# One stage instead of three behind the recurrent branch, and eight table loads moved from the opening stage into the first norm's stage

## The reference, cut to what matters

```
def rwkv_output(y, prep, r_k, gn_w, gn_b):
    r, k_mod, v, g = prep[0], prep[1], prep[2], prep[6]
    mu = jnp.mean(y, axis=-1, keepdims=True)
    var = jnp.mean(jnp.square(y - mu), axis=-1, keepdims=True)
    yn = ((y - mu) * lax.rsqrt(var + GN_EPS)).reshape(B, L, RWKV_WIDTH) * gn_w + gn_b
    coef = ...                      # one number per token and head
    bonus = (coef[..., None] * v.reshape(B, L, RWKV_HEADS, RWKV_HEAD)).reshape(B, L, RWKV_WIDTH)
    return (yn.astype(r.dtype) + bonus) * g       # g = sigmoid(gl) @ g2
```

## Time and profile before

| | |
|---|---|
| median of 3 runs | 3859.2 us (3856.57 to 3866.98) |
| the profiled execution's own time | 3855.86 us |
| its span, first to last instruction | 3854.0 us |
| TensorE busy | 3429.4 us (89%) |
| VectorE busy | 1710.8 us (44%) |
| ScalarE busy | 976.4 us (25%) |
| mean granted TensorE clock | 0.938 of full speed |

### The profile page before, as it was taken

The page is one execution under the profiler, slowest core; times in us unless marked ns, Lnnn a source line. Parts: engine busy times, 40 slices in busy tenths (PEclk is TensorE's granted clock), DMA queues, the critical chain, the costliest instruction groups (busy, mean ns, idle before and its releaser), DMA issues. The chain is left out here.

```text
span 3854.0 us, 66346 instructions
## 1 busy us (share of the span) xinstructions
PE 3429.4 (89%) x28910; PEld 2721.4 (71%) x28910; DVE 1710.8 (44%) x2845; ACT 976.4 (25%) x1671; POOL 38.9 (1%) x48
## 2 busy tenths in 40 slices
PE   5969997997988999996989977899999978979998
PEld 3858995766867655554845845788887867868877
DVE  3655554563155111113544437544443256555643
ACT  3035441242222111112111133311112132533322
POOL 0000000000000000000000000000000000000000
PEclk8969997998998899998999988999999989999999
DMA  6130002503255799994531100144432111013332
GB/s 241 61 137 4 4 4 97 192 23 111 83 181 196 303 410 411 410 414 155 181 113 49 55 14 22 61 115 121 125 114 72 61 31 50 1 45 99 98 105 87
DMA packets 254322, 486.84 MB, mean 126 GB/s; under 512 B 12394, under 2 KB 148107, under 8 KB 245364
## 3 DMA queue, kind: packets, MB, share of 16 engines
q1 hardware_dynamic: 246964, 457.91, 34.1%
q0 software_dynamic: 1984, 16.81, 1.1%
q10 hardware_dynamic: 5120, 8.39, 0.6%
HBM read 453.68 MB, written 29.39 MB: 125 GB/s over the span
## 5 line engine op out<-in xcount | busy, mean ns | idle before, releaser
L398 PE MATMUL banks<-leading,w_rest 128*128 128x512 f32 (+2 forms) x2016 | 733.8, 364 | 60.2 <-DVE w_rest L335 59.6
L398 PE MATMUL banks<-rest,w_leading 128*128 128x512 f32 (+2 forms) x2016 | 722.9, 359 | 0.0
L398 PE MATMUL banks<-leading,w_leading 128*128 128x512 f32 (+2 forms) x2016 | 721.2, 358 | 0.0
L335 DVE TENSOR_TENSOR w_rest<-land,w_leading 128x1024 fp32r<-128x1024 f32 (+2 forms) x344 | 321.7, 977 | 518.1 <-ACT w_leading L320 518.1
L398 PEld LDWEIGHTS banks<-leading,w_rest 128*128 128x128 f32 (+1 forms) x2016 | 383.5, 190 | 132.9 <-DVE w_rest L335 40.0
L320 ACT CAST w_leading<-land 128x1024 fp32r<-128x1024 f32 (+2 forms) x344 | 275.7, 849 | 709.1 <-DMA land<-in_w_in 245.1
L398 PEld LDWEIGHTS banks<-leading,w_leading 128*128 128x128 f32 (+1 forms) x2016 | 383.0, 190 | 57.4
L398 PEld LDWEIGHTS banks<-rest,w_leading 128*128 128x128 f32 (+1 forms) x2016 | 384.1, 191 | 54.1
L398 PE MATMUL banks<-w_rest,leading 128*128 128x512 f32 (+3 forms) x772 | 297.2, 385 | 51.6 <-DVE w_rest L335 51.6
L398 PE MATMUL banks<-w_leading,rest 128*128 128x512 f32 (+3 forms) x772 | 292.0, 378 | 0.0
L398 PE MATMUL banks<-w_leading,leading 128*128 128x512 f32 (+3 forms) x772 | 290.6, 376 | 0.0
(11 more groups left out here) (586 smaller groups left out, 5080.8 us busy)
## 6 DMA issues: line engine op xcount, KB each, us to landing
wg<-in_w_exp_gate SPq DMA_DIRECT2D x32, 2048.0 KB, 12.7
wu<-in_w_exp_up SPq DMA_DIRECT2D x32, 2048.0 KB, 14.8
wd<-in_w_exp_down SPq DMA_DIRECT2D x32, 2048.0 KB, 11.8
ws<-in_ada_w SPq DMA_DIRECT2D x96, 512.0 KB, 3.8
land<-in_w_in SPq DMA_DIRECT2D x41, 1024.0 KB, 5.5
land<-in_ffn_up SPq DMA_DIRECT2D x44, 512.0 KB, 5.3
land<-in_ffn_up SPq DMA_DIRECT2D x88, 256.0 KB, 3.3
ws<-in_w_ada SPq DMA_DIRECT2D x32, 512.0 KB, 3.8
```

The costliest lines, as they stand in the source:

```text
L335: nc.vector.tensor_tensor(rest[s % 2][:, k0:k1, 0:n], slots[s % wslots][:, k0:k1, 0:n], leading[s % 2][:, k0:k1, 0:n].bitcast(F32), ALU.su ...
L398: mm = nc.tensor.matmul(bank_of(r, kind, at), lhsT, rhs, start=(k == 0 and q == 0), stop=(k == kt - 1 and q == len(each) - 1))
```

## The change

The three result stages become one. What each engine's list holds now:

- TensorE: the four bonus products, then (after `g2` has landed) the four gate products, then, after VectorE has read the bonus products and normed `y`, the 16 transposes, head pair by head pair (four pieces fill one bank).
- VectorE: mean and centring in two halves of 1024 values, the sums of squares in two halves, then the four bonus multiplications, the scaling by `rstd` in two halves, and per head pair an addition and the gate multiplication.
- ScalarE: the squares in two halves (before, VectorE multiplied), the root, and the reading of the transposed heads with scale `gn_w` and bias `gn_b`, 128x512 at a time.
- GpSimd: both loads of `hT` one behind the other, and the wait for both.
- SyncE: the load of `g2`, for which TensorE now waits itself.

In the opening, SyncE no longer issues the eight tables; it does so at the start of its list in the first norm's stage and then waits for them.

```
@@ opening
                 bring_ahead(m, sp)
-                for dst, src in later:
-                    sp.dma_start(dst[:], src).then_inc(m.tables_sem, 16)
-                m.tables_count = 16 * len(later)
+                m.later_tables = later
@@ block_one
+        def tables(sp):
+            for dst, src in m.later_tables:
+                sp.dma_start(dst[:], src).then_inc(m.tables_sem, 16)
+            sp.wait_ge(m.tables_sem, 16 * len(m.later_tables))
...
-                   lambda sp: sp.wait_ge(m.tables_sem, m.tables_count), m.first_sums)
+                   tables, m.first_sums)
@@ rwkv_result
+        halves_of = [slice(groups * q, groups * (q + 1)) for q in range(2)]
...
             @block.gpsimd
-                pool.dma_start(m.hT[0][:, :, :], m.hT_dram[0]).then_inc(m.back, 16)
+                for part, x in enumerate(m.hT):
+                    pool.dma_start(x[:, :, :], m.hT_dram[part]).then_inc(m.back, 16)
+                pool.wait_ge(m.back, 32)
...
+            @block.tensor
+                for p in range(KB):
+                    mm = nc.tensor.matmul(m.ps[:, 4 + p, :], m.headspread[0:RH, p, :], m.coef[0:RH, :], start=True, stop=True)
+                    mm.then_inc(made_sem, 1)
+                pe.wait_ge(landed_sem, 16)
+                for p in range(KB):
+                    nc.tensor.matmul(m.ps[:, p, :], b.g2[:, p * P:(p + 1) * P], m.rw[:, 14, CTX:TOK], start=True, stop=True).then_inc(made_sem, 1)
+                pe.wait_ge(scaled_sem, KB)
+                pe.wait_ge(normed_sem, 2)
+                for h in range(KB):
+                    for t in range(NTL):
+                        mm = nc.tensor.transpose(m.ps[:, 4 + h, t * P:(t + 1) * P], m.y[:, t, h * P:(h + 1) * P], m.ident)
+                    mm.then_inc(turned_sem, 1)
             @block.scalar
+                for q, own in enumerate(halves_of):
+                    act.wait_ge(centred_sem, q + 1)
+                    nc.scalar.activation(b.sq[:, own, :], y[:, own, :], ACT.Square).then_inc(squared_sem, 1)
                 act.wait_ge(summed_sem, 1)
                 nc.scalar.activation(b.root[:, :], b.ss[:, :], ACT.Sqrt).then_inc(rooted_sem, 1)
+                for h in range(KB):
+                    act.wait_ge(turned_sem, h + 1)
+                    nc.scalar.activation(m.br_rw[:, h, :], m.ps[:, 4 + h, :], ACT.Identity, bias=gb[:, h:h + 1], scale=gw[:, h:h + 1]).then_inc(taken_sem, 1)
```

More of the change, by code:

```diff
@@ L1936, in rwkv_result @@
             nc, ctx, mean=[NTL * RH, 1], ss=[NTL * RH], root=[NTL * RH], rstd=[NTL * RH, 1], sq=[NTL * RH, HD], g2=[512], t=[KB, LAT])
+        groups = NTL * RH // 2
+        halves_of = [slice(groups * q, groups * (q + 1)) for q in range(2)]
         y = m.y[:].rearrange("p t (h e) -> p (t h) e", e=HD)
-        n = NTL * RH
-        with stage(nc, landed=1, summed=1, rooted=1, chain=1) as (block, landed_sem, summed_sem, rooted_sem, chain_sem):
+        gw, gb = cols(m, "gn_w"), cols(m, "gn_b")
+        with stage(nc, landed=1, centred=1, squared=1, summed=1, rooted=1, made=1, scaled=1, normed=1, turned=1, taken=1, chain=1) as (
+                block, landed_sem, centred_sem, squared_sem, summed_sem, rooted_sem, made_sem, scaled_sem, normed_sem, turned_sem, taken_sem, chain_sem):
             @block.gpsimd
             def _(pool):
-                pool.dma_start(m.hT[0][:, :, :], m.hT_dram[0]).then_inc(m.back, 16)
+                for part, x in enumerate(m.hT):
+                    pool.dma_start(x[:, :, :], m.hT_dram[part]).then_inc(m.back, 16)
+                pool.wait_ge(m.back, 32)
             @block.sync
@@ L1946, in _ @@
                 sp.dma_start(b.g2[:, :], a["gate_w2"]).then_inc(landed_sem, 16)
-                sp.wait_ge(landed_sem, 16)
+            @block.tensor
+            def _(pe):
+                for p in range(KB):
[10 more added lines that the diff above has]
+                    mm.then_inc(turned_sem, 1)
             @block.scalar
             def _(act):
+                for q, own in enumerate(halves_of):
+                    act.wait_ge(centred_sem, q + 1)
+                    nc.scalar.activation(b.sq[:, own, :], y[:, own, :], ACT.Square).then_inc(squared_sem, 1)
                 act.wait_ge(summed_sem, 1)
                 nc.scalar.activation(b.root[:, :], b.ss[:, :], ACT.Sqrt).then_inc(rooted_sem, 1)
+                for h in range(KB):
+                    act.wait_ge(turned_sem, h + 1)
+                    nc.scalar.activation(m.br_rw[:, h, :], m.ps[:, 4 + h, :], ACT.Identity, bias=gb[:, h:h + 1], scale=gw[:, h:h + 1]).then_inc(taken_sem, 1)
             @block.vector
@@ L1956, in _ @@
                 chain = Chain(dve, chain_sem)
[L1957 to L1961, removed]
+                for own in halves_of:
+                    chain(nc.vector.tensor_reduce(b.mean[:, own, 0], y[:, own, :], AX, ALU.add))
+                    chain(nc.vector.tensor_scalar(b.mean[:, own, 0], b.mean[:, own, 0], 1.0 / HD, None, ALU.mult))
+                    nc.vector.tensor_tensor(y[:, own, :], y[:, own, :], bc(b.mean[:, own, :], HD), ALU.subtract).then_inc(centred_sem, 1)
@@ L1962, in _ @@
+                for q, own in enumerate(halves_of):
+                    dve.wait_ge(squared_sem, q + 1)
+                    chain(nc.vector.tensor_reduce(b.ss[:, own], b.sq[:, own, :], AX, ALU.add))
                 nc.vector.tensor_scalar(b.ss[:, :], b.ss[:, :], 1.0 / HD, GN_EPS, ALU.mult, ALU.add).then_inc(summed_sem, 1)
+                for p in range(KB):
+                    dve.wait_ge(made_sem, p + 1)
+                    nc.vector.tensor_tensor(b.t[:, p, :], m.ps[:, 4 + p, :], m.rw[:, 8 + p, CTX:TOK], ALU.mult).then_inc(scaled_sem, 1)
@@ L1963, in _ @@
                 dve.wait_ge(rooted_sem, 1)
                 chain(nc.vector.reciprocal(b.rstd[:, :, 0], b.root[:, :]))
[L1965 to L1988, removed]
@@ new lines, in _ @@
+                for own in halves_of:
+                    nc.vector.tensor_tensor(y[:, own, :], y[:, own, :], bc(b.rstd[:, own, :], HD), ALU.mult).then_inc(normed_sem, 1)
+                dve.wait_ge(made_sem, 2 * KB)
+                dve.wait_ge(scaled_sem, KB)
+                for h in range(KB):
+                    dve.wait_ge(taken_sem, h + 1)
+                    chain(nc.vector.tensor_tensor(b.t[:, h, :], b.t[:, h, :], m.br_rw[:, h, :], ALU.add))
+                    chain(nc.vector.tensor_tensor(m.br_rw[:, h, :], b.t[:, h, :], m.ps[:, h, :], ALU.mult))
```

## The result

The changed kernel takes 3838.95 us (median of 4 runs, 3838.54 to 3840.92) against 3860.61 us for the kernel before (4 runs, 3856.57 to 3866.98): ratio 0.9943, 95% interval 0.9931 to 0.9955. Measured a second time (experiment 10) it took 3840.88 us beside 3861.29, ratio 0.9949 (0.9936 to 0.9963). The medians differ by 21.7 and 20.4 us. The two profiled executions, 3855.86 us before and 3839.17 after, differ by 16.7.

What follows compares the result with a forecast made beforehand. Bound: barriers waiting for SyncE's tables in the opening and the result stages' serial chain. -3.5 - 16.2 = -19.7 us gives 3836.2 from the profiled time, 3839.5 from the median; forecast 3838, range 3829 to 3848.

Steps and rivals of the forecast that it cites:

- Part 1: Opening: moving SyncE's eight table issues into the first norm's stage starts that stage 3.5 us earlier, loads covered there.
- VectorE's path: Result stage: norm in halves, bonus multiplications and scaling end at 636.4 us, when the transposes may start.
- TensorE's path: Result stage: eight bonus and gate products, the clock falling at 624.5, end at 636.8 us, at most 638.9.
- as low as 630: Result stage: TensorE's products end this early if the clock stays up or comes back during the four gate products.
- Rival B: Result stage: clock stays low, TensorE is the bound, transposes from 638.9; in all -17.7 us, about 3840; chance 0.10.
- The pair of loads: Result stage: GpSimd's two hT loads, one behind the other, the second landing at 644.5 us, bounds 642.8 to 647.0.
- the lower bound's reading: Pair of hT loads: if the copy's 1 MB neighbour was all in between, the second load lands at 642.8 us.
- Rival A: Result stage: the two loads don't overlap, land at 647.0 and are the bound; -17.2 us, about 3840.5; chance 0.20.
- The wait that was hidden becomes the last one: Result stage's end: loads and VectorE end within half a microsecond, 644.5 against 644.2, so the load wait comes last.
- Rival C: Opening: the tables don't pay, 0 us for moving them; 3842 to 3843 us; chance 0.08.
- E: Whole kernel: nothing measurable, since waits elsewhere soak up the gain; chance 0.07.
- D: Result stage: g2 lands behind the pair and delays the gate products; slower once it lands after 648.6; chance 0.03.

Runs made afterwards that it cites:

- experiment 10: The changed kernel once more, unchanged, on the same chip as experiment 9; 3840.88 us, ratio 0.9949.
- experiment 2: The changed kernel with the eight table loads put back at the end of the opening; 3842.99 us, ratio 0.9953.
- experiment 5: The changed kernel with SyncE instead of GpSimd issuing the two 3 MB loads, right behind the g2 load; 3840.66 us, ratio 0.9947.
- experiment 6: The changed kernel with VectorE reading the transposed heads from the banks itself and ScalarE adding the bias to the bonus earlier; 3843.5 us, ratio 0.9956.
- experiment 7: The changed kernel with both edits: SyncE issues the two loads and VectorE reads the banks itself; 3839.82 us, ratio 0.9945.
- experiment 1: The kernel before with only the eight table loads moved into the first norm's stage; 3857.11 us, ratio 0.9993.
- experiment 8: The changed kernel with g2 issued by GpSimd as a third load behind the two 3 MB loads; 3853.36 us, ratio 0.9979.
- experiment 4: The kernel before once more, unchanged, for a second profile; 3857.99 us.
- experiment 9: The kernel of experiment 7 once more, beside the changed kernel on the same chip; 3841.49 us, ratio 0.995.
- experiment 3: The changed kernel with the bonus and gate products, and VectorE's bonus multiplications, placed behind the transposes; 3847.12 us, ratio 0.996.

## Why the prediction was right

The predicted 3838 us is 1 us from the 3838.95 measured, and the range (3829 to 3848) holds it. That nearness is partly luck. The gain by the medians is 21.7 us, not 19.7, the kernel before came out 1.4 us above the median I started from, and I had put the forecast between its profiled time and that median. What held is the mechanism and the size of each part. Step by step, in us from the start of the result stage:

| Step | predicted | measured |
|---|---|---|
| Tables out of the opening | -3.5 | -3.4 (means of 3 and 9 profiles) |
| Sums of squares done | 8.0 | 7.9 |
| Scaling done | 13.6 | 12.95 |
| TensorE's products done | 13.8 (7.2 to 16.1) | 8.95 |
| VectorE's last part begins | 15.6 | 14.75 |
| VectorE's last part | 5.8 | 5.75 |
| VectorE ends | 21.4 | 20.50 |
| Second load landed | 21.7 (20.0 to 24.2) | 20.6 |
| Barrier | 0.9 | 0.74 |
| Stage | 22.6 | 21.24 |

- **Part 1** held as written. The wait goes, the loads go under the norm's stage, and that stage does not get longer.
- **VectorE's path** held to 0.9 us. The four bonus multiplications follow each other at 0.60 us, not the 0.69 of a single row (629.40 to 631.79), and the two scalings take 2.36, not 2.5.
- **TensorE's path was mis-sized**, though it did not set the end. I let the clock fall at 624.5, as it had in the earlier trace rows with TensorE idle. With the bonus products running it stayed at full (2.4 GHz) until about 624.9, was at half until about 628.3, and came back during the gate products, as the windows in the last section show: the case that the prediction named with "as low as 630". The price at half clock was too high as well: I took 2.01 us from products that alternate between the two kinds, and products of one kind behind each other take 1.70 (last section). Rival B, in which it stays down, did not come about: the products were done 4 us before VectorE let the transposes go (2.45 us before in experiment 2).
- **The pair of loads** lands 17.4 us after the first issue (18.4 in experiment 2), where I took 18.5 out of bounds of 16.8 and 21.0. So the lower bound's reading fits better, that the 1 MB beside the copy in the earlier trace rows took most of the time by which that pair was longer; the copy's first part alone took 11.4 us, where the load's takes 10.0, and no run took the 1 MB away. The Trainium skill ("DMA: Bandwidth & Descriptors", Anatomy of one DMA) would have it, as an estimate from its formula, at 16.4: nearer than my 18.5 by a hair, 1.0 us short instead of 1.1 long. Rival A, no overlap at all, is out: the second takes 16.8 from its own issue, not 20.4.
- **"The wait that was hidden becomes the last one"** is half the truth. It becomes one of two; experiments 5 to 7 show it, and in experiment 2 it is the last.
- **Rival C** is out by experiment 1's profiles, **E** by the ratios, and **D** by `g2` landing in 2.5 us; experiment 8 made D on purpose and its path came out at 13.8 us where I had 16.5, since the clock rose during the products. By that path `g2` would have to land after 651.3, not 648.6, before the whole were slower.

What is not settled: in the profiled pair the two parts make 2.7 + 17.6 = 20.3 us, of which 16.7 are left at the end, while the medians differ by 20.4 to 21.7. The profile of before was also quicker than each of the four runs of its kernel taken for the result. Stretches that no kernel changed differ by up to 3 us between executions. The scan is one. Another begins at 872 us in the kernel before and ends some 68 us later: it lasts 67.7 to 68.5 us in before, after and experiments 1, 4 and 9, and 70.8 to 71.7 in the others. The kernel alone doesn't decide it, since experiments 7 and 9 run one kernel, and so do after and experiment 10. But seven of the nine profiles with one result stage have the longer form and none of the three with three stages, so a part that the change plays in it isn't ruled out. And at the scan's start the kernels with the tables moved are 4.9 us ahead by the means (227.1 against 231.9), 1.5 more than at the norm's stage; the stretch between has overlapping lengths in the two groups (188.3 to 190.5 against 190.0 to 191.3). What sets these differences was not tested.

## What to carry to other kernels

A TensorE that is 89% busy says nothing about a stage in which it waits: lay out each barrier and ask which engine's last row comes last, since such time comes off the total in full. Put work whose inputs are ready early (here products that need nothing of the norm) ahead of the engine's own wait, and issue the small load it needs ahead of the big ones: the same 256 KB took 2.5 us in front of 6 MB and 17.1 behind it. When a stage gets shorter, look for the chain that ties next; for two chains that end within 0.2 us, shorten each and then both: only both together gave the 1.7 us here.

## What the runs showed of the hardware

**The granted clock of a stretch can't be read off what TensorE does in it.** Windows of the changed kernel (stretch, its us, busy us and count by engine, granted clock, DMA share, GB/s):

```profile
624.00:625.00 1.00, 1.00 (x3) 0.18 (x1) 1.00 (x2) 0.70 (x1) 0.19 (x1) 0.93 0.00 0
625.00:626.00 1.00, 1.00 (x2) 0.50 (x2) 0.93 (x3) 0.35 (x1) 0.94 (x2) 0.50 0.00 0
...
629.00:630.00 1.00, 1.00 (x4) 0.38 (x2) 0.96 (x4) 0.48 (x2) 0.00 (x0) 1.00 0.98 418
631.00:632.00 1.00, 0.00 (x0) 0.00 (x0) 1.00 (x3) 0.00 (x0) 0.00 (x0) 1.00 0.93 393
...
636.00:637.00 1.00, 1.00 (x7) 1.00 (x6) 0.67 (x1) 0.92 (x2) 0.00 (x0) 0.50 1.16 492
...
639.00:640.00 1.00, 0.00 (x0) 0.00 (x0) 0.93 (x3) 0.00 (x0) 0.00 (x0) 1.00 0.98 418
```

TensorE works without a pause from 621.58 to 630.5, and the clock falls to half (1.2 GHz) in the middle of it and comes back. It falls again during the transposes, after 4 us of idleness at full clock, and TensorE idles from 638.0 while the clock goes back to full at 638.5. So the level in one window is no image of what TensorE does in it, and a burst of some microseconds can cost the price of either level: the 16 transposes took 3.27 us here, 1.91 in experiment 8 at full clock, where products ran right ahead of them, and 3.67 in experiment 3 at half, after 12 us of idleness. The products too: they rose to full after about 3 us in the changed kernel and after 5 in experiment 8, and in experiment 3 never:

```profile
644.00:648.00 4.00, 4.00 (x6) 0.99 (x5) 2.07 (x3) 0.00 (x0) 0.00 (x0) 0.50 0.00 0
...
648.00:652.00 4.00, 4.00 (x5) 0.94 (x4) 2.07 (x3) 0.00 (x0) 0.00 (x0) 0.50 0.00 0
```

There TensorE was busy for all of the 16 us at clock 0.50, as in the earlier trace rows. The Trainium skill ("TensorE: Matmul & The Clock Gate", What's actually happening) lets activity release the throttle. The rise at 628.3, with products running, agrees; the rise at 638.5 with TensorE idle, experiment 3 and the earlier trace rows don't. What sets these two apart from the changed kernel's products no run here tells.

**A product with 8 rows costs what one with 128 costs.** In experiment 3, at half clock, the bonus product takes 2.07 us and the gate product 2.08.

**At half clock, products of one kind behind each other are cheaper than alternating ones.** Each product has two records, each with a weight load. In experiment 8 four gate products follow each other, and while the clock is at half their weight loads start 0.85 us apart, 1.70 per product:

```profile
641.38 0.34 PEld L1961 LDWEIGHTS banks<-rw,g 128*128 128x128 f32 x1 [0.52 <-issue]
642.23 0.34 PEld L1961 LDWEIGHTS banks<-rw,g 128*128 128x128 f32 x1 [0.52 <-issue]
643.09 0.34 PEld L1961 LDWEIGHTS banks<-rw,g 128*128 128x128 f32 x1 [0.52 <-issue]
```

In experiment 3 gate and bonus products take turns, and so they do in the kernel before; a product starts every 2.0 us at the same clock:

```profile
637.93 0.50 PEld L1967 LDWEIGHTS banks<-rw,g 128*128 128x128 f32 x2 [1.50 <-issue]
639.93 0.50 PEld L1966 LDWEIGHTS banks<-coef,headspread 8*128 8x128 f32 x2 [1.50 <-issue]
```

Whether the change of kind is the cause no run tested by itself.

**The issuing engine made no difference to the pair.** From GpSimd the loads land in 10.0 to 10.4 and 16.8 to 17.8 us (six profiles), from SyncE in 9.8 to 10.2 and 16.6 to 17.0 (three). What SyncE buys is the 3.2 us that GpSimd needs before it issues.
